# PEER layer of a two-block transformer: expert gates built by one-hot products, against gates scatter-added to a DRAM matrix

## What is computed

```
q = (x @ wq).reshape(T, 8, 2, 128)
s = einsum('thcd,ckd->thck', q, subkeys)
sv, si = top_k(s, 16)
cand = sv[:, :, 0, :, None] + sv[:, :, 1, None, :]
cv, ci = top_k(cand.reshape(T, 8, 256), 16)
ea, eb = si[:, :, 0][ci // 16], si[:, :, 1][ci % 16]
experts = ea * 128 + eb            # gate = softmax(cv) per head
y = sum over picks of gate * gelu(x . u[expert]) * v[expert]
x = layer_norm(ALPHA * x + y)
```

## Time and profile before

| | us |
|---|---|
| median of three runs | 3106.95 (3103.88 to 3107.64) |
| profiled execution, span | 3103.2 |
| PE busy | 3057.2 (99% of the span) |
| PE weight load busy | 2554.6 (82%) |
| DVE busy | 2046.3 (66%) |
| ACT busy | 1443.2 (47%) |
| POOL busy | 169.3 (5%) |

### The profile page before, as it was taken

One profiled execution on the slowest core, in us unless ns is written; L12 is line 12 of the kernel. 1 busy time (PEld: TensorE's weight loads), 2 busy tenths in 40 slices (PEclk: granted clock), 3 DMA queues, 4 the chain that ended last, 5 costly groups with the idle time before them and its releaser, 6 DMA issues.

```text
span 3103.2 us, 46862 instructions
## 1 busy us (share of the span) xinstructions
PE 3057.2 (99%) x15988; PEld 2554.6 (82%) x15988; DVE 2046.3 (66%) x4032; ACT 1443.2 (47%) x2280; POOL 169.3 (5%) x305
## 2 busy tenths in 40 slices
PE   8999999999999999999999999999999999999999
PEld 6688876868887688899888888888989988888887
DVE  5577752546774352898777677765289976777776
ACT  2436642335663243156355555544315635555554
POOL 3110000200000000410000000000042000000000
PEclk9999999999999999999999999999999999999999
DMA  8758897745889632433655555553243266555554
GB/s 323 260 187 315 299 351 272 281 131 191 310 300 348 234 120 91 140 100 102 199 195 190 192 190 191 190 170 139 90 137 109 90 196 198 192 191 190 190 189 142
DMA packets 167142, 614.74 MB, mean 198 GB/s; under 512 B 18752, under 2 KB 18784, under 8 KB 166096
## 3 DMA queue, kind: packets, MB, share of 16 engines
q1 hardware_dynamic: 151632, 551.62, 51.9%
q0 software_dynamic: 15360, 61.16, 5.2%
HBM read 611.66 MB, written 1.05 MB: 197 GB/s over the span
## 4 chain that ended last, share of the span: by engine, by line
PE 94%; DVE 3%; ACT 1%; DMA 1%; issue 0%; DVEq 0%; POOL 0%; ACTq 0%; SPq 0%; POOLq 0%
PE PS L1660 13%; PE PS L1661 12%; PE PS L1662 12%; PE PS L2311 11%; PE PS L1706 7%; PE PS L2271 6%; PE PS L2313 6%; PE PS L2192 5%; PE PS L2294 4%; PE PS L1720 2%; PE PS L1747 2%; PE PS L1981 2%; PE PS L2177 2%; PE PS L2030 1%; PE PS L2303 1%; DVE gu_lo L1253 1%
## 5 line engine op out<-in xcount | busy, mean ns | idle before, releaser
L627 ACT ACTIVATE w_hi<-arena 128x1024 fp32r<-128x1024 f32 x448 | 473.0, 1057 | 178.8 <-PE PS L1662 107.8
L1030 DVE TENSOR_TENSOR w_lo<-arena,w_hi 128x1024 fp32r<-128x1024 f32 x448 | 530.7, 1220 | 2.2 <-ACT w_hi L627 0.2
L1660 PE MATMUL PS<-w_hi,pw_hi 128*128 128x512 f32 x1024 | 401.5, 392 | 0.2 <-DVE pw_lo L1605 0.2
L1661 PE MATMUL PS<-w_lo,pw_hi 128*128 128x512 f32 x1024 | 400.7, 391 | 0.0
L1662 PE MATMUL PS<-w_hi,pw_lo 128*128 128x512 f32 x1024 | 398.4, 389 | 0.0
L2311 PE MATMUL PS<-x_lh,w_hi 128*128 128x512 f32 x1536 | 379.4, 389 | 0.0
L2311 PEld LDWEIGHTS PS<-x_lh,w_hi 128*128 128x128 f32 x1536 | 288.2, 188 | 59.8
L1253 DVE TENSOR_TENSOR gu_lo<-raw,gu_hi 128x1024 fp32r<-128x1024 f32 x192 | 222.9, 1221 | 18.5 <-ACT gu_hi L719 18.4
L973 ACT ACTIVATE arena<-PS 128x256 f32<-128x256 f32 x192 | 73.9, 385 | 343.9 <-PE PS L2313 343.9
L1662 PEld LDWEIGHTS PS<-w_hi,pw_lo 128*128 128x128 f32 x1024 | 192.3, 188 | 41.6
L2271 PE MATMUL PS<-x,arena 128*128 128x256 f32 x896 | 223.2, 380 | 0.0
(11 more groups left out here) (420 smaller groups left out, 5250.6 us busy)
## 6 DMA issues: line engine op xcount, KB each, us to landing
arena<-in_u_t SPq DMA_DIRECT2D x256, 512.0 KB, 3.4
arena<-in_v_t SPq DMA_DIRECT2D x256, 512.0 KB, 4.5
raw<-in_w_gu SPq DMA_DIRECT2D x192, 512.0 KB, 5.4
arena<-in_w SPq DMA_DIRECT2D x152, 512.0 KB, 3.6
arena<-in_w_ada POOLq DMA_DIRECT2D x96, 512.0 KB, 7.3
raw<-in_w_down SPq DMA_DIRECT2D x96, 512.0 KB, 5.6
arena<-in_w_gu SPq DMA_DIRECT2D x64, 512.0 KB, 7.0
arena<-in_w_down SPq DMA_DIRECT2D x32, 512.0 KB, 5.1
```

Of the source, the lines that this page charges most:

```text
L627: A(w_hi[:, m % RING], ring[:, m % RING], ACT.Copy).then_inc(S["hi_done"], 1)
L1030: V.tensor_tensor(w_lo[:, m % RING], ring[:, m % RING], w_hi[:, m % RING].bitcast(F32), ALU.subtract)\
L1660: mm(dst, w[0], m[0], start=start, stop=False, skip_group_check=skip)
L1661: mm(dst, w[0], m[1], start=False, stop=False, skip_group_check=skip)
```

## The change

What the new code does, in the order of the program:

- **nsa stage.** POOL clears a piece of SBUF and writes it as zeros to a DRAM matrix `g_dram[l]` of 16384 x 256 fp32 (16.8 MB), in 16 DMAs of 1 MB (`g_zero`), on its own queue between the stage's small loads and the peer layer's keys.
- **Routing.** DVE does POOL's part too (multiply, one reduction) and forms the row number of each pick in `g_dram`: (eb * 128 + ea) * 256 + token. The gates are made per head; ACT's exponentials stand at places written out by hand (`EXPS_IN_Q`, `EXPS_IN_UP`), among the native products' gelus.
- **Scatter.** For each head and each half of the tokens, POOL issues 16 indirect DMAs of 128 one-element rows, with addition (`peer_gates`): 256 in a layer. Before those of a head it waits for the same half of the head before.
- **First products.** 24 in native form (`NATIVE`), the residual, then 104 split ones in a row. gelu results stay in SBUF (`HID`, 128 blocks).
- **Second products.** 128 in a row; the last four first products (`SWAP`) alternate with the first four second ones. SP waits for all scatters (`g_put`) before it loads the first of these slots, then loads the gates two blocks at a time (256 KB, 64 in a layer) from `g_dram`, between the weights. ACT rounds the gated result (`first_hi`), DVE multiplies and forms the rest.

The diff, cut to its core:

```diff
-EARLY, EARLY_1, LATE = 32, 17, 4
+NATIVE = 24
+STEP = 4
+PEER_UP = PK - NATIVE
+EXPS_IN_Q = {3: 0, 6: 1, 8: 2}
+EXPS_IN_UP = {2: 3, 7: 4, 12: 5, 16: 6, 22: 7}
+SWAP = 4
+ZERO_N = 16
...
+        ids = arena[:, RING_AT + 12800:RING_AT + 12800 + PAIRS_N].bitcast(U32)
+        gate = arena[:, RING_AT + 13056:RING_AT + 13056 + PAIRS_N]
+        g_dram = [nc.dram_tensor(f"g_dram{l}", (PK * PK * T, 1), F32).ap() for l in range(DEPTH)]
...
+        HID = arena[:, 0:T * PK].rearrange("p (b t) -> p b t", t=T)
+        gbuf = HID[:, PK - SWAP:].rearrange("p (k b) t -> p k b t", b=2)
...
(SP)
+                with sp.Fori(1, PEER_UP // STEP - 1) as i:
+                    for j in range(STEP):
+                        u(n + j, i * STEP + (NATIVE + j), i, 1)
+                for t in range(TT):
+                    sp.wait_ge(g_put[t], 16 * PH * TOPK * (l + 1))
+                for b in range(SWAP):
+                    if b < 2:
+                        g(b, b, PK * l if l else None)
+                    v(n + down_slot(b), b)
+                    u(n + down_slot(b) + 1, PK - SWAP + b)
+                n += PEER_UP
+                with sp.Fori(1, PK // STEP) as i:
+                    for j in range(STEP):
+                        v(n + j, i * STEP + j, i, 1)
+                        if j % 2:
+                            g(i * (STEP // 2) + j // 2, j // 2, i * STEP + (PK * l + j - 3))
...
(POOL)
-            def peer_ids(l):
+            def g_zero(l):
+                nc.gpsimd.memset(zero, 0.0).then_inc(S["zero_ok"], 1)
+                pool.wait_ge(S["zero_ok"], l + 2)
+                dst = g_dram[l].rearrange("(c p r t) o -> c p r (t o)", c=ZERO_N, p=P, t=2 * T)
+                for c in range(ZERO_N):
+                    pool.dma_start(dst[c], zero.unsqueeze(1).to_broadcast([P, 4, 2 * T])).then_inc(S["g_zero"], 16)
+            def peer_gates(l):
+                pool.wait_ge(S["g_zero"], 16 * ZERO_N * (l + 1))
+                for hd in range(PH):
+                    pool.wait_ge(S["pk_ok"], PH * l + hd + 1)
+                    for t in range(TT):
+                        if l + hd:
+                            pool.wait_ge(g_put[t], 16 * TOPK * (PH * l + hd))
+                        for k in range(TOPK):
+                            n = HEAD_N * hd + TOPK * t + k
+                            pool.indirect_dma_start(out=g_dram[l], out_offset=bass.IndirectOffsetOnAxis(ap=ids[:, n:n + 1], axis=0),
+                                                    in_=gate[:, n:n + 1], in_offset=None, compute_op=ALU.add).then_inc(g_put[t], 16)
...
(ACT, second products)
+                def first_hi(b, j):
+                    act.wait_ge(S["ag_ok"], b + (PK * l + 1))
...
+                    A(pw_hi[:, j % 2], hidden(b), ACT.Copy).then_inc(S["pw_first"], 1)
...
(DVE, routing of a head)
+                    for c in range(2):
+                        for t in range(TT):
+                            e = Q["eq"][:, c, TOPK * t:TOPK * t + TOPK]
+                            V.tensor_tensor(e, e, Q["si"][:, t, 2 * hd + c].unsqueeze(1).to_broadcast([P, TOPK, TOPK]), ALU.mult)
+                    dve.drain()
+                    V.tensor_reduce(Q["ab"], Q["eq"], AX.X, ALU.add)
...
+                    V.scalar_tensor_tensor(ids[:, HEAD_N * hd:HEAD_N * hd + HEAD_N], Q["idf"], float(T), token[:], ALU.mult, ALU.add)
...
(DVE, second products)
+                def weighted(b, j, i):
+                    dve.wait_ge(S["gelu_ok"], b + (PK * l + 1))
+                    if j % 2 == 0:
+                        dve.wait_ge(g_load[j // 2 % 2], 16 * i + (16 * (PK // 4 * l + j // 4 + 1)))
+                    V.tensor_tensor(hidden(b), hidden(b), gbuf[:, j // 2 % 2, j % 2], ALU.mult).then_inc(S["ag_ok"], 1)
+                def rest(b, j):
+                    dve.wait_ge(S["pw_first"], b + (PK * l + 1))
+                    V.tensor_tensor(pw_lo[:, j % 2], hidden(b), pw_hi[:, j % 2].bitcast(F32), ALU.subtract).then_inc(S["pw_ok"], 1)
...
(PE)
-                for i in range(T):
...
-                    mm(PS[:, 4 + i // 4 % 4, P * (i % 4):P * (i % 4) + P], OA[:, i % GDEEP], OB[:, i % GDEEP], start=True, stop=True)\
-                        .then_inc(S["pt_mm"], 1)
-                    if gate_product(i):
-                        early_up(*gate_product(i))
...
+                for j in range(STEP):
+                    up(j, j, first=True)
+                with pe.Fori(1, PEER_UP // STEP - 1) as i:
+                    for j in range(STEP):
+                        up(STEP * i + j, j, i, 1)
+                for b in range(SWAP):
+                    down(b, b, slot=down_slot(b))
+                    up(PEER_UP - SWAP + b, b, slot=down_slot(b) + 1)
+                with pe.Fori(1, PK // STEP - 1) as i:
+                    for j in range(STEP):
+                        down(STEP * i + j, j, i, 1)
```

More of the change, by code:

```diff
@@ L976, in peer @@
-                split_hi(("peer", l), EARLY)
-                step(0, True)
-                with act.Fori(1, (PK - EARLY) // PEER_STEP - 1) as i:
-                    step(i, False)
-                step((PK - EARLY) // PEER_STEP - 1, False, last=True)
+                    A(HID[:, e], PS[:, native_bank(e), 0:T], ACT.Gelu_apprx_tanh).then_inc(S["gelu_ok"], 1)
+                    if e in EXPS_IN_UP:
+                        exps(EXPS_IN_UP[e])
+                    if 0 <= e - (NATIVE - 4) < 3:
+                        split_hi(s, e - (NATIVE - 4))
@@ new lines, in ups @@
+                def ups(i, last=False):
+                    for j in range(STEP):
+                        e = STEP * i + j
+                        split_hi(s, 3 + j, i, 1)
+                        if not (isinstance(i, int) and i == 0 and j == 0):
+                            gelu(e - 1, j + 1)
+                        if last and j == STEP - 1:
+                            first_hi(0, 0)
+                        lo_half(e, j)
+                ups(0)
+                with act.Fori(1, PEER_UP // STEP - 2) as i:
+                    ups(i)
@@ L1532, in peer, with routing @@
                 hk = lambda w: w.rearrange("p (h k) -> p h k", k=TOPK)
-                for hd in range(PH):
+                def routing(hd):
                     dve.wait_ge(S["ps_ev"], PH * l + hd + 1)
@@ new lines, in peer @@
+                if l == 0:
+                    dve.wait_ge(S["zero_ok"], 1)
+                for hd in range(PH):
+                    routing(hd)
+                    if hd:
+                        gates(hd - 1)
+                gates(PH - 1)
+                split_lo(q, 0)
+                split_lo(q, 1)
+                dve.wait_ge(S["slot_done"], n0)
+                for k in range(KT):
+                    if k % 4 == 0:
+                        dve.wait_ge(S["res_ok"], 2 * l + k // 4 + 1)
+                    V.tensor_tensor(x_lo[:, k], x[:, k], x_hi[:, k].bitcast(F32), ALU.subtract).then_inc(S["xs_ok"], 1)
@@ new lines, in peer @@
+                ups(0)
+                with dve.Fori(1, PEER_UP // STEP - 2) as i:
+                    ups(i)
+                ups(PEER_UP // STEP - 2, True)
+                for b in range(SWAP):
+                    split_lo(q, down_slot(b) + 2)
+                    weighted(b + 1, b + 1, 0)
+                    rest(b + 1, b + 1)
+                    split_lo(q, down_slot(b) + 3)
+                    if b == SWAP - 1:
+                        weighted(b + 2, b + 2, 0)
+                    total(PEER_UP - SWAP + b, b)
@@ new lines, in downs @@
+                def downs(i, last=False):
+                    for j in range(STEP):
+                        b = STEP * i + j
+                        if not (last and j == STEP - 1):
+                            rest(b + 1, j + 1)
+                        if not (last and j >= 2):
+                            split_lo(q, PEER_UP + 2 + j, i, 1)
+                            weighted(b + 2, j + 2, i)
+                downs(1)
+                with dve.Fori(2, PK // STEP - 2) as i:
+                    downs(i)
@@ L1646, in peer @@
+                downs(PK // STEP - 2)
+                downs(PK // STEP - 1, True)
                 layer_norm(l, 1)
@@ L2304, in peer, with up @@
                     last.then_inc(S["slot_done"], 1)
-                n0 = BASE_SPLIT["peer", l]
-                def up(n, j, b, i=0, per=0):
-                    pe.wait_ge(S["gelu_ok"], PK * l + b - 3)
+                pe.wait_ge(S["gelu_ok"], PK * l + NATIVE - 4)
+                for half in range(2):
+                    residual(1, half).then_inc(S["res_ok"], 1)
+                n0 += NATIVE
+                def up(e, j, i=0, per=0, first=False, slot=None):
+                    if first:
+                        pe.wait_ge(S["gelu_ok"], PK * l + NATIVE - 4 + j + 1)
+                    else:
+                        pe.wait_ge(S["up_sum"], e + (PEER_UP * l - 3))
+                    n = n0 + (j if slot is None else slot)
```

396 lines of the change are left out of this document (126 added, 270 removed).

## The result

| | before | changed |
|---|---|---|
| median of four runs | 3105.41 us (3101.76 to 3107.64) | 3389.86 us (3388.32 to 3391.0) |
| span of the profiled execution | 3103.2 | 3387.8 |

The changed kernel is **slower**, at 1.0914 of the time before (95% interval 1.0899 to 1.093). I had forecast 2978.

A forecast was written before the change was run, and what follows sets the result against it. PE, with 94% of the chain of waits, was taken as the bound: 787.35 - 722.9 saves 64.5 us a layer, 129 in both, so 3103.2 - 129 = 2974 of span, plus 3.75, forecast 2978; range 2962 to 3190.

The forecast's parts named there:

- I take twice that row, 1.1 us: POOL's scatters: one indirect DMA priced at twice a direct DMA issue's 0.53 us; 256 take 282 us, done about 1561.
- the 1.44 allowed: Scatters of a layer: 369 us from start to last permitted issue, for 256 scatters, so 1.44 us each.
- the port: Split first products: a scatter waiting out DVE's weight split loses 0.27 us on average, so 1.1 becomes 1.37.
- Rival A: POOL is the bound: scatters over 1.44 us delay second products, 2978 + 512 x (t - 1.44); chance 0.22 slower, 0.11 below break-even.
- deadline: Layer 0's last scatter must be issued by 1646 so the second products' first slot is ready; lateness costs in full, twice.
- PE's sum: PE's work in a peer layer: natives 82.9, residual 1.7, split first products 287.0, second products 348.7, together 720.3 us.
- t = 1.85: t is one scatter's time in us; the forecast range's slow end took it up to 1.85, giving 3190.
- zeros in nsa: Writing 2 x 16.8 MB of zeros while weights load: costed at nothing; some 10 us a layer if a slot came late.
- the gates' way back: Second products load gates from DRAM at 241 GB/s against 373 shown: nothing, if landing grows by no more than 3.
- B: DMA engines are the bound: scatter packets at 170 ns make each layer 163 us late, 3304; decides from 90 ns; chance 0.07.
- C: Scatters in time, but a product stage steps slower, 0.2 us a product: 3029; chance 0.08, still faster than before.
- D: Native products wait for ACT's exponentials; a head's routing of 18 us delays the seam 14 a layer, 3006; chance 0.04.

The follow-up runs named there:

- run with the operand in PSUM: Against the changed kernel, DVE's weight split in the split first products subtracts PSUM data instead of the rounded weights (one SBUF input, wrong result): 3210.77 us, 1.0339 of before.

## Why the prediction was wrong

**The step that failed: "I take twice that row, 1.1 us".** A scatter's own time, which I took as twice the direct issue, measured 1.85, and that is 0.41 over the 1.44 allowed, not 0.34 under it. My range for it (0.53 to 2.3) held it, and I had chosen the lower end as "nearer" because the number of descriptors is the same. The runs show that this was the wrong likeness: a scatter hardly depends on the rows (0.15 of 1.85 for 64 rows). It is mostly a fixed price of another instruction: 1.27 for the index form with a plain write, 0.58 more for the addition. Neither had a row in the trace, and a factor of two over the nearest row stood on nothing. What POOL does in that time stays open. With this term alone right, 105 us a layer would have been late (256 x 0.41), 210 in all, a time near 3190. The run with the operand in PSUM is about this case: 3211.

**The second term, the port, was of the right kind and a third of its size.** I had the mechanism: DVE's split in the first products, 1.22 of 2.76 us, holds a scatter up. But 0.44 x 0.61 = 0.27 is the mean for starts that fall at random. They don't: POOL works without a pause, a held scatter is released about at the split's end, and from there the 1.42 that remain, the 0.30 and the next split's start set the next meeting, just behind that start. The hold was 0.94 for most of the 100 scatters in that stage, 0.91 on average over its steps, and it costs 179 us of the 403.

**Rival A's formula held; that the deadline fits to 2 us is luck in part.** Last issue allowed by 1646, and what comes later costs its lateness in full: 200.7 late by that, 199.1 idle on PE. But two terms of the deadline were off and cancel: the first products ended at 1662.15 where I had 1655.4, and from the last issue to PE's restart it took 14.55 us where landing, load and splits had come to 9.1. With the mean distance measured, (1846.72 - 1279.74) / 255 = 2.22, rival A gives 2978 + 512 x 0.78 = 3377; the 9 us of PE's sum and the 5 of the clock, both below, make up the rest to 3390. It had 0.22, with 0.48 for the forecast. The range ended at t = 1.85, which happens to be the quiet value; nothing in it stood for the port on top of a large own time.

**PE's sum held.** Natives and residual 84.8 us where I had 84.6; DVE's routing over at 1377.7 where I had 1375.8; 1.74 us of wait at the seam; second products at 2.72. Without the scatters it is 2986.58 against 2978, and the first products are where that lies: from the first split one to the first second one PE took 280.8 us in layer 0 of that run (1381.34 to 1662.11) and 282.1 in layer 1, where I had 276. The step was 2.79 and not 2.76, and the first ones of the stage were longer. Up to the first split product 0.9 and 0.3 us were gained.

**Costed at nothing, and rightly:** zeros in nsa (the first native product starts at 1294.17, against 1292.28 before, and anywhere from 1290.31 to 1295.10 in the other runs with the zeros) and the gates' way back. B (the DMA engines) falls: the same packets pass 179 us sooner once DVE's operand is elsewhere, and in the hole the share is 0.25. From 1660 to 1847 POOL's queue moved 14410 packets in 22.3% of the engines' time, 46 ns each, where B needed about 90. C and D did not come about.

**One cost not foreseen:** after 199 us of idle time PE's clock is at its lower level (0.51 granted in the hole), and the first second product takes 2.6 us more in layer 0 and 2.0 in layer 1, 5 in both.

## What to carry to other kernels

When a change puts an instruction on the critical path of which the trace has no row, don't price it by a likeness to a neighbour. Work out the price at which the change breaks even, here 1.44 us, and look at how little it takes to be over it; then measure that one instruction alone before the rest is built. And where two engines contend for something in a loop, don't take the mean wait: draw two or three rounds, ask where the next start falls after a held one, and whether the rhythm locks. If a scatter must add, see whether its additions can be made ahead by an engine that has time; a plain one took two thirds here (1.27 of 1.85).

## What the runs showed of the hardware that was not expected

- An indirect DMA of 128 one-element rows keeps POOL busy 0.97 us with a plain write and 1.55 with an addition, with 0.30 before the next in both; a direct issue took 0.53. With 64 rows they are 0.89 and 1.40.
- A DVE instruction with two SBUF inputs holds such a scatter only at its start, and only if DVE was first: a scatter that starts up to 0.06 us ahead of the split, or up to 0.04 behind its start, goes through and runs on beside DVE; one that starts 0.06 or more behind loses what is left of the split, less 0.13 or 0.14.
- Through this the two engines lock: at 1.85 for a scatter one fits into a step of 2.79, at 1.70 three fit into two, at 1.27 two fit into one.
- The additions did not slow the weights: the DMA engines' share from 1384 to 1660 was 0.58 without scatters, 0.62 with plain ones, 0.68 with adding ones and 0.74 with adding ones 1.86 apart (the run with the operand in PSUM), and `in_u_t` landed in 3.5 us without scatters, 3.5 or 3.6 with them.
